# A hybrid decoder step on one core: block choice moved into the attention, half of the samples' key scores moved to VectorE, and half of their pages fetched earlier

## What is computed

```python
s_c = einsum('nqhd,ncd->nqhc', q, kc) * scale        # 127 compressed keys
p_c = masked_softmax(s_c, cvalid)                    # softmax over the keys that end before q
o_c = einsum('nqhc,ncd->nqhd', p_c, vc)
p_sel = block_importance(p_c.sum(axis=2), ns)        # 32 blocks of 64 tokens, weights .5 1 1 1 .5
forced = valid & ((j == 0) | (j > cur - SEL_LOCAL))  # first block and the last two always
_, idx = lax.top_k(where(forced, inf, where(valid, p_sel, -inf)), 16)
o_s = attention over the tokens of the 16 chosen blocks
o_w = attention over the last 512 tokens
return gates[0] * o_c + gates[1] * o_s + gates[2] * o_w
```

## Time and profile before

| | |
|---|---|
| median of 3 runs | 2122.35 us (2118.34 to 2126.47) |
| profiled execution, its own time | 2121.0 us |
| its span | 2119.4 us |
| PE busy | 1888.1 us (89%) |
| DVE busy | 1066.8 us (50%) |
| ACT busy | 617.2 us (29%) |
| choice stage, span's 1134 to 1253 us | PE 80.31, DVE 79.29, ACT 48.51 us busy |
| attention stage, 1253 to 1714.5 us | PE 425.57, DVE 231.27, ACT 151.19 us busy |
| sample attention, 1714.5 to 1903 us | PE 149.54, DVE 41.33, ACT 1.63 us busy |

### The profile page before, as it was taken

One profiled execution on the slowest core, in us unless ns is written; L12 is line 12 of the kernel. 1 busy time (PEld: TensorE's weight loads), 2 busy tenths in 40 slices (PEclk: granted clock), 3 DMA queues, 4 the chain that ended last, 5 costly groups with the idle time before them and its releaser, 6 DMA issues. The chain is left out here.

```text
span 2119.4 us, 24335 instructions
## 1 busy us (share of the span) xinstructions
PE 1888.1 (89%) x8663; PEld 1347.0 (64%) x8663; DVE 1066.8 (50%) x2180; ACT 617.2 (29%) x1112; POOL 148.8 (7%) x256
## 2 busy tenths in 40 slices
PE   6699999999999999929996848899999977877999
PEld 1588878877877787626556533444454457775886
DVE  1377538755864685435465665555555322213332
ACT  3324443434343432214212512233333310002110
POOL 2101110000000000022300000000000021000000
PEclk9799999999999999958996757999999965557999
DMA  7537555545454644326213000000000032005431
GB/s 242 181 119 235 181 193 203 183 144 185 159 196 168 195 167 156 119 83 180 75 45 98 24 21 16 10 11 11 5 11 1 0 111 76 18 13 192 137 131 57
DMA packets 139671, 230.60 MB, mean 109 GB/s; under 512 B 14439, under 2 KB 91913, under 8 KB 139080
## 3 DMA queue, kind: packets, MB, share of 16 engines
q1 hardware_dynamic: 110677, 158.88, 23.5%
q0 software_dynamic: 17296, 56.70, 7.4%
q10 hardware_dynamic: 11579, 13.48, 2.0%
HBM read 175.27 MB, written 56.15 MB: 109 GB/s over the span
## 5 line engine op out<-in xcount | busy, mean ns | idle before, releaser
L613 PE MATMUL ps<-h_hi,w_hi 128*128 128x512 f32 x832 | 341.6, 411 | 0.6 <-DMA w_lo<-split_weights 0.6
L615 PE MATMUL ps<-h_lo,w_hi 128*128 128x512 f32 x832 | 325.4, 391 | 0.0
L614 PE MATMUL ps<-h_hi,w_lo 128*128 128x512 f32 x832 | 325.1, 391 | 0.0
L2151 PE MATMUL ps<-pT,values 128*65 128x512 f32 x412 | 216.3, 608 | 0.0
L2213 ACT ACTIVATE pT<-ps 128x512 f32<-128x512 f32 x206 | 123.0, 597 | 294.5 <-PE ps L2138 196.2
L2293 DVE TENSOR_REDUCE part_max<-ps 128x1 f32<-128x512 f32 (+3 forms) x272 | 143.1, 557 | 123.0 <-PE ps L2166 49.1
L955 DVE SCALAR_TENSOR_TENSOR c_acc<-c_u,par,c_acc 128x512 f32<-128x512 f32 x240 | 180.2, 751 | 6.8
L613 PEld LDWEIGHTS ps<-h_hi,w_hi 128*128 128x128 f32 x832 | 157.3, 189 | 36.8 <-issue 7.3
L614 PEld LDWEIGHTS ps<-h_hi,w_lo 128*128 128x128 f32 x832 | 157.3, 189 | 36.2 <-issue 6.3
L615 PEld LDWEIGHTS ps<-h_lo,w_hi 128*128 128x128 f32 x832 | 156.7, 188 | 34.0
L1375 PE MATMUL ps<-rawT,x_in 128*128 128x254 f32 (+1 forms) x320 | 137.5, 590 | 0.0
(11 more groups left out here) (594 smaller groups left out, 3138.9 us busy)
## 6 DMA issues: line engine op xcount, KB each, us to landing
w_hi<-split_weights SPq DMA_DIRECT2D x78, 512.0 KB, 3.7
w_lo<-split_weights SPq DMA_DIRECT2D x78, 512.0 KB, 4.6
w_raw<-in_w_in SPq DMA_DIRECT2D x26, 512.0 KB, 4.5
split_weights<-w_hi POOLq DMA_DIRECT2D x26, 512.0 KB, 5.5
split_weights<-w_lo POOLq DMA_DIRECT2D x26, 512.0 KB, 6.2
x_in<-in_x_prompt SPq DMA_DIRECT2D x4, 2048.0 KB, 10.5
tm<-in_x_prompt SPq DMA_DIRECT2D x16, 512.0 KB, 4.7
out_y_prompt<-y_out SPq DMA_DIRECT2D x16, 512.0 KB, 2.9
```

What stands on the lines that cost most here:

```text
L613: m.matmul(out, w_hi[:, b, kk, :], hh[:, kk, :], start=(kk == 0), stop=False)
L614: m.matmul(out, w_lo[:, b, kk, :], hh[:, kk, :], start=False, stop=False)
L615: return m.matmul(out, w_hi[:, b, kk, :], hl[:, kk, :], start=False, stop=(kk == KT - 1))
L2151: m.matmul(k.ps[0:VW, 5 + b, :], k.va[:, t, b, :], pT[:, i % NPT].rearrange("p h q -> p (h q)"), start=first, stop=end).then_inc(z["pv_don ...
```

## The change

Three parts.

1. **Choice stage.** Queries, `cs` and `mx` get three buffers instead of two. DVE's order in step s is now `mask(s-1)`, `normalise(s-3)`, PE's is `scores(s-1)`, `turn(s-3)`, `values(s-4)` and the gate. The head sum is made only for blocks 8 to 15. The two 2 MB loads of gate weights are issued after the third and fourth query load. The choosing at the end is gone.
2. **Attention stage.** For blocks qb of 8 and more a step `pick` does the choosing for one block, two query blocks ahead, behind the third score tile; it is a `misc` step (DVE, then one PE transpose, then a DVE copy). For blocks 0 to 7 the bias is set to zero. SP issues the 64 page loads of samples 0, 1, 4, 5, sixteen behind the query loads of blocks 3, 7, 11, 15.
3. **Sample attention.** The keys of samples 4 to 7 are no longer turned: DVE multiplies each landed page with the query spread over 128 partitions and sums over the 64 columns (16 times a product and a reduction of 1024 elements). For that DVE builds `spread_q`, PE makes two 512-column matmuls from it, ACT copies them to `wide_q`; 16 small matmuls give these samples' bias and one DVE addition joins both. The copies to `kT` of the other 24 batches go to ACT. Only samples 2, 6, 3, 7 are still fetched in this stage, in this order.

```diff
@@ stage_choice @@
-                if b >= 2:
-                    sp.wait_ge(z["sc_done"], b - 1)
+                if b >= 3:
+                    sp.wait_ge(z["sc_done"], b - 2)
...
-            for s in range(NC + 3):
-                for step, b in ((scores, s - 1), (turn, s - 2), (values, s - 3)):
+            for s in range(NC + 4):
+                for step, b in ((scores, s - 1), (turn, s - 3), (values, s - 4)):
...
-            for s in range(NC + 3):
-                for step, b in ((normalise, s - 2), (mask, s - 1)):
+            for s in range(NC + 4):
+                for step, b in ((mask, s - 1), (normalise, s - 3)):
@@ stage_attention @@
+                if n == 2 and FREE <= qb + 2 < NC:
+                    order.append(("pick", qb + 2))
...
+                if qb % 4 == 3:
+                    n = EARLY[qb // 4]
+                    landed = sem(f"early_pages{n}")
+                    for g in range(PAGES):
+                        load_page(k, sp, n, g, landed)
...
+                elif step == "pick":
+                    pe.wait_ge(z["chosen"], qb - FREE + 1)
+                    last = m.transpose(bank[0:NBLK, 0:P], imp[:, qb % 2, :], k.ident[:, :])
...
+                link(v.max(m8[:, 0:8], e))
+                link(v.match_replace(spare[:, :], m8[:, 0:8], e, -3e38))
+                link(v.max(m8[:, 8:16], spare[:, :]))
+                link(v.match_replace(rest[:, :], m8[:, 8:16], spare[:, :], -3e38))
+                v.tensor_scalar(e, rest[:, :], -2e38, NEG, ALU.is_gt, ALU.mult).then_inc(z["chosen"], 1)
@@ stage_sample_attention @@
+            for half in range(2):
+                act.wait_ge(z["wide"], half + 1)
+                nc.scalar.copy(wide_q[:, 2 * half:2 * half + 2].rearrange("p n h d -> p (n h d)"), k.ps[:, 2, :]).then_inc(z["wide_cp"], 1)
...
+            for g in range(PAGES):
+                last = m.matmul(B4[:, :, g, :], kT[HD:HD + NBLK, g * P:(g + 1) * P], qT[HD:HD + NBLK, N0:NS, :], start=True, stop=True)
...
+                    link(v.tensor_tensor(tile, at.rearrange("p g (o d) -> p g o d", o=1).broadcast_to([P, 4, H, HD]),
+                                         wide_q[:, i].rearrange("p (o h) d -> p o h d", o=1).broadcast_to([P, 4, H, HD]), ALU.mult))
+                    link(v.tensor_reduce(part[:, i, 4 * b4:4 * b4 + 4, :], tile, AX.X, ALU.add))
```

More of the change, by code:

```diff
@@ L1896, in scores @@
                 for h in range(H):
-                    last = m.matmul(k.ps[:, 2 + b % 2, h * P:h * P + M], qf[:, b % 2, h, :], k.kcT[:, 0, 0:M], start=True, stop=True)
+                    last = m.matmul(k.ps[:, 2 + b % 2, h * P:h * P + M], qf[:, b % 3, h, :], k.kcT[:, 0, 0:M], start=True, stop=True)
                 last.then_inc(z["sc_done"], 1)
@@ L1929, in _ @@
                     gate(s - 8)
[L1930 to L1933, removed]
         @block.scalar
@@ L1957, in _ @@
             act.wait_ge(z["va_done"], 1)
-            for s in range(NC + 3):
-                for step, b in ((exps, s - 1), (probs, s - 2), (share, s - 3)):
+            for s in range(NC + 4):
+                for step, b in ((exps, s - 1), (probs, s - 3), (share, s - 4)):
                     if 0 <= b < NC:
@@ L2106, in stage_attention @@
         MISC = 7
-        MISC_STEPS = ("shift", "part_sel", "part_win", "out")
+        MISC_STEPS = ("shift", "part_sel", "part_win", "out", "pick")
         misc_at = {step: n + 1 for n, step in enumerate(s for s in order if s[0] in MISC_STEPS)}
@@ L2391, in _ @@
             m.matmul(k.ps[0:HD, 7, 0:96], one[0:NS, 0:HD], gd[:, :, :].rearrange("a n g -> a (n g)"), start=True, stop=True).then_inc(z["tr0"], 1)
+            for half in range(2):
+                pe.wait_ge(z["spread"], 1)
+                if half:
+                    pe.wait_ge(z["wide_cp"], 1)
+                m.matmul(k.ps[:, 2, :], one[0:HD, :], spread_q[:, 2 * half:2 * half + 2].rearrange("k n h d -> k (n h d)"),
+                         start=True, stop=True).then_inc(z["wide"], 1)
             pe.wait_ge(z["cp0"], 2)
@@ L2420, in pool_values @@
             def pool_values(b, G, v):
+                if b == 0:
+                    for n in range(N0, NS):
+                        wait_pages(pe, n)
                 pe.wait_ge(z["exd2"], b + 1)
@@ L2426, in pool_values @@
                     for g in range(G):
-                        last = m.matmul(k.ps[0:HD, 7, n * H:(n + 1) * H], v[:, n, g, :], p4[:, n, g, :], start=(g == 0), stop=(g == G - 1))
+                        last = m.matmul(k.ps[0:HD, 7, n * H:(n + 1) * H], v(n, g), p4[:, n, g, :], start=(g == 0), stop=(g == G - 1))
                 last.then_inc(z["av"], 1)
-            NE = 4 * NS + NS
+            NE = len(batches)
             def keys(e):
-                if e < 4 * NS:
-                    n, b4 = divmod(e, 4)
-                    for landed, share in zip(kin[n], shares):
-                        pe.wait_ge(landed, 16 * len(share))
-                    src = [pages[:, n, 4 * b4 + t, 0:HD] for t in range(4)]
+                kind, n, b4 = batches[e]
+                if kind == "sel":
+                    wait_pages(pe, n)
+                    src = [sample_page(k, n, 4 * b4 + t)[:, 0:HD] for t in range(4)]
                 else:
                     pe.wait_ge(z["win_in"], 16 * NS)
-                    src = [win[:, e - 4 * NS, t, 0:HD] for t in range(4)]
+                    src = [win[:, n, t, 0:HD] for t in range(4)]
                 if e >= 2:
@@ L2480, in _ @@
             last.then_inc(z["cp0"], 1)
+            dve.wait_ge(z["cp0"], 1)
+            for n in range(ND):
+                last = v.tensor_tensor(spread_q[:, n], k.ident[0:HD, 0:HD].rearrange("k (o d) -> k o d", o=1).broadcast_to([HD, H, HD]),
+                                       qT[0:HD, N0 + n, :].rearrange("k (h o) -> k h o", o=1).broadcast_to([HD, H, HD]), ALU.mult)
+            last.then_inc(z["spread"], 1)
             v.tensor_copy(newT[:, :, :].rearrange("d i n -> d (i n)"), k.ps[0:HD, 6, Q:2 * Q]).then_inc(z["cp0"], 1)
```

186 lines of the change are left out of this document (106 added, 80 removed).

## The result

The changed kernel takes 2158.64 us in the median of four runs (2153.75 to 2164.92), the kernel before 2121.27 beside it; the ratio is 1.0172, 95% interval 1.0149 to 1.0195. The prediction was 2139 in a range of 2102 to 2162: the direction was right and the time inside the range, but the slowdown is twice the one forecast.

| stage, from its first instruction | before | after | difference | forecast |
|---|---|---|---|---|
| choice stage | 118.3 | 141.5 | +23.2 | +17.6 |
| attention stage | 461.8 | 520.1 | +58.2 | +44.8 |
| sample stage, to the first reduction | 136.1 | 88.9 | -47.1 | -45.7 |

A forecast was written before the change was run, and what follows sets the result against it. It took a PE-DVE ring to bound the choice stage, PE the attention, and page fetching with PE the sample stage before; 2121.0 + 17.6 + 44.8 - 45.7 = 2137.7, so 2139 against the median, range 2102 to 2162.

The forecast's parts named there:

- the ring: Choice stage: list order makes PE and DVE alternate, 7.65 us a step without gate; attention starts 17.6 us later.
- gate steps: Choice stage, eight steps with gate: 9.3 us each, the middle of 7.35 at full clock and 11.3 at half.
- The Trainium skill's rule on loops: Choice stage rival: matmuls between waits run cold, gate steps wholly at 1.2 GHz; choice +34, total 2155, chance 0.13.
- Attention, the wait: Attention, each of eight picks: PE stands 3.9 us at the pick's transpose until DVE has chosen.
- the early loads: Attention: SP's early page loads take 18 us behind a query load wanted over a block later, costing nothing.
- Attention, the clock: Attention, each pick: a lowered clock after the wait costs PE 1.7 us more; 44.8 us for eight picks with the wait.
- The high end of 58: Attention: upper end of the slowdown over eight picks, 58 us, with two losses of clock a pick.
- Sample stage: Sample stage: longer head, then 24 key batches without waits for DMA; the softmax starts 45.7 us earlier, ends 42 to 49.
- Sixteen bias matmuls: Sample stage: weight loads cost by columns, 7.2 us in all; by rows 2.4; keys start at 1742.7.
- the rival of a sample stage bound by DVE: Sample stage: a broadcast operand costs DVE double, ending at 1825 and not 1805; total 2158, chance 0.05.
- ring open: Choice stage: scores get ahead of the turn, steps bound by PE alone; total near 2095, chance 0.07.
- picks hidden: Attention: DVE is done choosing before PE arrives, 44.8 falls to under 10; total 2103, chance 0.06.

The follow-up runs named there:

- c1: Changed kernel with DVE running normalise(s-3) ahead of mask(s-1) in each step of the choice stage: 2103.44 us, ratio 0.9907.
- c2: Changed kernel with eleven useless PE matmuls ahead of the transposes in the eight choice-stage steps with gate: 2138.25 us, ratio 1.0072.
- p2: Changed kernel with twelve useless PE matmuls just ahead of each pick's transpose in the attention: 2126.99 us, ratio 1.0023.
- b1: Changed kernel with normalise ahead of mask, choosing in four pieces behind tiles 3 to 6, and PE's transpose behind tile 7: 2042.57 us, ratio 0.9633.
- p4: Changed kernel with nine of DVE's eleven instructions of each pick left out, so blocks chosen aren't the best: 2126.79 us, ratio 1.0016.
- p3: Changed kernel with the choosing left whole behind the third tile, PE's transpose of it behind the fifth: 2133.69 us, ratio 1.0047.

## Why the prediction was right in direction and half the size

- **Choice stage, the ring: right.** Steps without gate were 7.65 forecast and 7.53 measured; PE waits 2.7 us in each, 2.8 to 2.9 forecast. c1 shows that the order of DVE's list is the cause.
- **Choice stage, gate steps: mis-sized.** "I take the middle of 7.35 and 11.3, 9.3" is one of the two terms that failed: they take 10.2, 7.1 us more over eight steps, partly made up by steps without gate and an end that are shorter, so that the stage is 5.6 us over its forecast. Halfway between the clocks was a guess on a quantity that has two levels. The profile of before had the means to do better: behind a gap the clock was at half for two thirds of the five us that followed. Two thirds of the way from 7.35 to 11.3 is 10.0, an estimate from one gap, but close to the 10.2 measured. With the gap filled (c2) the step is 7.15. The Trainium skill's rule on loops (TensorE: Matmul & The Clock Gate, section "Loop structure matters more than you think"), weighed as a rival, has a long wait for DMA before every matmul, behind which they run cold. Here the wait is 2.7 us and for DVE; the trace agrees for all of the step but the scores at its end.
- **Attention, the wait: right**, 3.9 forecast, 3.95 measured, eight times; the early loads cost nothing, as said.
- **Attention, the clock: mis-sized, and the largest part of the error.** In "Per pick 3.9 + 1.7 = 5.6" the 1.7 is the other term that failed: the clock costs 2.8 a pick (22.4 by p2), 8.8 us more over eight picks. 1.7 came from one dip of 3.4 us behind one gap; I took the one dip that I had looked at as the size of all, although the attention of before opens with 27.3 us at half clock. At these stops the clock was at half for up to 13.6 us, 7.2 in the mean. The high end of 58 had two dips of 3.4 a pick, which is nearly what came.
- **The error in full.** The sum gave 2137.7 and the profiled execution took 2153.75, 16.1 more. Of these 8.8 are the clock at the picks and 5.6 the choice stage; 2.0 more come at the picks (waits of 31.6 for 31.2, and 1.6 that p2 has too), 2.6 in the attention ahead of them and not from the picks, and 2.8 go the other way (sample stage, and the choice stage's start). The median lies another 4.9 above the profiled execution; the mean granted clock of the four executions falls as their time rises, from 0.880 at 2153.75 us to 0.876 at 2164.92, but in which stage is on record for the profiled one alone.
- **Sample stage: right**, -47.1 for -45.7. Sixteen bias matmuls take 6.98 us (7.2 forecast by columns; by rows it would have been 2.4), keys start after 27.6 us (28.0), and DVE's product and reduction take 1.22 us each where I had put down 1.38, well inside PE's time (DVE waits 27 us at the end). So the rival of a sample stage bound by DVE falls too.
- **The rivals of the faster side** (ring open, picks hidden) describe b1: each was real, and what kept it from this kernel is the order of two lists.

The sum by its own steps: 2121.0 + 23.2 + 58.2 - 47.1 - 1.4 = 2153.9, measured 2153.75.

What stays open: what decides whether and for how long the clock goes down at a stop. Equal waits of 3.95 us came with 3.4 to 13.7 us at half clock, and c1 and c2, with the same picks, lost 6 to 8 us more in their profiled attention than the changed kernel did. Nor is it the length of one stop alone. The dip of the earlier trace rows began in the second of these two stops in the kernel before, of 1.30 and 0.87 us, while p2's stops of 1.16 had none:

```profile
1289.41 0.60 PE L2182 MATMUL ps<-ident,row_shift 128*2 128x128 f32 x4 [1.30 <-DVE row_shift L2246]
1290.88 0.77 PE L2137 MATMUL ps<-q_hi,keys_sel_masked 98*128 98x512 f32 x1 [0.87 <-DVE q_hi L2250]
```

## What to carry to other kernels

When two engines hand blocks to each other, write down for each list what stands ahead of the instruction that the other waits for: a buffer more and a longer lag help only if the older block's work stands ahead of the newer one's. Work put into an engine with room should come in pieces that its neighbours don't notice (here four of about 0.6 us cost next to nothing, one of 2.5 us made PE wait at the row maxima), and the consumer's instruction should stand well behind it. Price a new stop of PE as the wait and the clock with it, here 2.8 to 4.1 us beside a wait of 3.95, and test such a price by filling the stop with useless matmuls: that removes the clock's share alone.

## What the runs showed of the hardware

- Useless matmuls in a wait made the kernel faster: by 31.6 us in the median in p2, by 20.4 us in c2. The stop costs through the granted clock even where the time of the wait itself can't be had back.
- At the picks, stops of 1.16 us went with a dip in none of eight cases (p2), of 1.8 us in five of eight (p4), of 1.7 to 2.1 us in six of eight (p3), of 3.95 us in eight of eight (changed kernel). These are counts at this place; in the early attention of the kernel before a dip began in the second of two stops of 1.30 and 0.87 us.
- In the gate steps the clock was at 2.4 GHz while PE stood (1.00 from 1189 to 1190) and at 1.2 GHz while it worked (0.50 from 1191 to 1193), except for the scores. A steady alternation of work and stops, here 7.5 and 2.7 us, had the clock the wrong way round in seven steps on end.
